# Layer norms of a two-block float32 network: order of the mean matmuls on TensorE and of the mean subtraction on VectorE

## What is computed

```python
def layer_norm(x, g, b):
    mu = jnp.mean(xf, axis=-1, keepdims=True)
    xc = xf - mu
    var = jnp.mean(xc * xc, axis=-1, keepdims=True)
    y = xc * lax.rsqrt(var + LN_EPS) * g + b
```

## Time and profile before

| | |
|---|---|
| Time, median of 3 executions | 1786.06 us (1785.59 to 1788.69) |
| Time of the profiled execution | 1788.76 us |
| Its span | 1787.0 us |
| Mean granted TensorE clock | 0.989 |
| TensorE matmul busy | 1742.0 us (97%) |
| VectorE busy | 1210.3 us (68%) |
| ScalarE busy | 978.1 us (55%) |
| GpSimd busy | 114.7 us (6%) |

### The profile page before, as it was taken

The page is one execution under the profiler, slowest core; times in us unless marked ns, Lnnn a source line. Parts: engine busy times, 40 slices in busy tenths (PEclk is TensorE's granted clock), DMA queues, the critical chain, the costliest instruction groups (busy, mean ns, idle before and its releaser), DMA issues.

```text
span 1787.0 us, 33465 instructions
## 1 busy us (share of the span) xinstructions
PE 1742.0 (97%) x11768; PEld 1579.9 (88%) x11768; DVE 1210.3 (68%) x2117; ACT 978.1 (55%) x1708; POOL 114.7 (6%) x124
## 2 busy tenths in 40 slices
PE   8999998999999999999899998999999999999998
PEld 7888998888899888888788888889999998888887
DVE  6776788777554776677777756776656467777764
ACT  5564595655355554466565635564434364565543
POOL 0001003000100000100300010003000100030001
PEclk9999999999999999999999999999999999999999
DMA  6665365456545666443446652433556534346662
GB/s 222 187 205 194 118 202 167 145 188 207 188 133 175 189 187 206 147 124 125 160 161 188 209 184 72 136 116 109 166 175 202 171 101 129 116 127 196 188 204 88
DMA packets 76640, 290.79 MB, mean 163 GB/s; under 512 B 9345, under 2 KB 11649, under 8 KB 76545
## 3 DMA queue, kind: packets, MB, share of 16 engines
q1 hardware_dynamic: 76544, 289.50, 51.1%
HBM read 288.42 MB, written 1.05 MB: 162 GB/s over the span
## 4 chain that ended last, share of the span: by engine, by line
PE 87%; DVE 5%; ACT 2%; issue 2%; POOL 2%; DMA 0%; SPq 0%; POOLq 0%; ACTq 0%; DVEq 0%
PE psum L518 33%; PE psum L519 17%; PE psum L510 10%; PE psum L512 10%; PE psum L511 10%; POOL sums L1059 2%; PE psum L650 1%; PE psum L759 1%; DVE r L1708 1%; PE psum L645 1%; DVE wlo L1554 1%; PE psum L882 1%; PE psum L889 1%; DVE r L1739 1%; ACT whi L1093 0%
## 5 line engine op out<-in xcount | busy, mean ns | idle before, releaser
L1554 DVE TENSOR_TENSOR wlo<-raw,whi 128x1024 fp32r<-128x1024 f32 (+3 forms) x496 | 648.0, 1314 | 292.4 <-ACT whi L1093 291.2
L518 PE MATMUL psum<-x_split,whi 128*128 128x512 f32 x1760 | 618.5, 395 | 6.0 <-DVE x_split L1589 3.4
L1093 ACT ACTIVATE whi<-raw 128x1024 fp32r<-128x1024 f32 (+3 forms) x496 | 548.7, 1119 | 40.0 <-PE psum L512 21.1
L519 PE MATMUL psum<-x_split,wlo 128*128 128x256 f32 x1760 | 494.3, 281 | 0.0
L518 PEld LDWEIGHTS psum<-x_split,whi 128*128 128x128 f32 x1760 | 331.0, 188 | 84.8 <-issue 3.6
L510 PE MATMUL psum<-x_split,whi 128*128 128x272 f32 (+1 forms) x1184 | 346.6, 293 | 4.4 <-DVE x_split L1744 4.4
L512 PE MATMUL psum<-x_split,wlo 128*128 128x272 f32 (+1 forms) x1184 | 338.5, 286 | 0.0
L511 PE MATMUL psum<-x_split,whi 128*128 128x272 f32 (+1 forms) x1184 | 337.6, 285 | 0.0
L519 PEld LDWEIGHTS psum<-x_split,wlo 128*128 128x128 f32 x1760 | 331.5, 188 | 0.0
L518 PE MATMUL psum<-h_split,whi 128*128 128x512 f32 x770 | 272.2, 397 | 0.0
L510 PEld LDWEIGHTS psum<-x_split,whi 128*128 128x128 f32 x1184 | 223.3, 189 | 14.7 <-issue 8.2
(11 more groups left out here) (231 smaller groups left out, 1748.0 us busy)
## 6 DMA issues: line engine op xcount, KB each, us to landing
raw<-w_in SPq DMA_DIRECT2D x264, 512.0 KB, 3.5
raw<-w_out SPq DMA_DIRECT2D x96, 704.0 KB, 4.3
raw<-w_mix SPq DMA_DIRECT2D x44, 512.0 KB, 3.6
raw<-w_rg SPq DMA_DIRECT2D x25, 512.0 KB, 4.1
raw<-w_q SPq DMA_DIRECT2D x24, 512.0 KB, 3.6
raw<-w_mixo SPq DMA_DIRECT2D x16, 576.0 KB, 3.7
raw<-w_kv SPq DMA_DIRECT2D x16, 512.0 KB, 3.6
raw<-w_rg_out SPq DMA_DIRECT2D x8, 640.0 KB, 4.1
```

Source lines behind the costliest of these rows:

```text
L518: nc.tensor.matmul(ps[:, bank, :], whi[slot][:, w], split, start=start, stop=False)
L519: return nc.tensor.matmul(part(bank, 0), wlo[slot][:, w], split[:, 0], start=False, stop=stop)
L1093: nc.scalar.activation(whi[slot][:, 0:cols], raw[slot][:, 0:cols], ACT.Copy).then_inc(w_hi_done, count)
L1554: V.tensor_tensor(wlo[slot][:, 0:cols], raw[slot][:, 0:cols], f(whi[slot][:, 0:cols]), ALU.subtract).then_inc(w_lo_done, 1)
```

## The change

On TensorE the token means now come first and in one run; the two means of all partitions come behind them, in the place of the six keep_warm matmuls (emb keeps its own order). On VectorE the centrings are in five parts instead of four: tile 0, tile 1, tiles 2 and 3, 4 and 5, 6 and 7. No centring stands ahead of the variance any more; centre(0) comes behind the reciprocal, and each of the others directly behind the scaling of the last tile of the part before it. Each scaling waits for its own part's centring. The counts that others wait for change from 4 to 5 a norm, and GpSimd and TensorE wait once more for work of the norm before.

```diff
+CENTRE_PARTS = ((0, 1), (1, 2), (2, 4), (4, 6), (6, 8))
+CENTRES = len(CENTRE_PARTS)
+CENTRE_OF = [c for c, (first, end) in enumerate(CENTRE_PARTS) for _ in range(first, end)]
...
             if name == "emb":
-                pe.wait_ge(xc_done, 4 * n)
+                pe.wait_ge(xc_done, CENTRES * n)
...
             else:
                 pe.wait_ge(sums_done, norm_stages.index(name) + 1)
-                means(sums[:, 0, :], first=True)
                 token_means(sums[:, 0, :], 0)
                 token_means(sums[:, 1, :], 4)
 
                 pe.wait_ge(acc_free, by_name[name].u0 + by_name[name].units)
-                means(r[:, KD - 1, :], last=True).then_inc(mean_done, 1)
                 token_means(r[:, KD - 1, :], 0)
                 pe.wait_ge(sq_done, KD * (n + 1))
                 ins = token_means(sq[:, KD - 1, :], 4, True)
             ins.then_inc(stat_done, 1)
-            keep_warm(6)
+            if name == "emb":
+                keep_warm(6)
+            else:
+
+                if n:
+                    pe.wait_ge(xc_done, CENTRES * n)
+                means(sums[:, 0, :], first=True)
+                means(r[:, KD - 1, :], last=True).then_inc(mean_done, 1)
             pe.wait_ge(rstd_done, n + 1)
...
                 pool.wait_ge(stat_done, n)
+                pool.wait_ge(mean_done, n)
...
-                    act.wait_ge(xc_done, 4 * n + k // 2 + 1)
+                    act.wait_ge(xc_done, CENTRES * n + CENTRE_OF[k] + 1)
...
-            def centre(k):
-
-                mean = acc(4, T).unsqueeze(1).broadcast_to([P, 2, T])
-                V.tensor_tensor(r[:, k:k + 2, t], r[:, k:k + 2, t], mean, ALU.subtract).then_inc(xc_done, 1)
-
-            dve.wait_ge(mean_done, n + 1)
+            def centre(c):
+
+                k, end = CENTRE_PARTS[c]
+                mean = acc(4, T).unsqueeze(1).broadcast_to([P, end - k, T])
+                V.tensor_tensor(r[:, k:end, t], r[:, k:end, t], mean, ALU.subtract).then_inc(xc_done, 1)
+
             if name == "emb":
-                for k in range(0, KD, 2):
-                    centre(k)
+                dve.wait_ge(mean_done, n + 1)
+                for c in range(CENTRES):
+                    centre(c)
...
             else:
-                centre(0)
-
                 ns = norm_stages.index(name)
...
             V.reciprocal(rstd_t[:, 0:nt], std_t[:, 0:nt]).then_inc(rstd_done, 1)
             if name != "emb":
-                centre(2)
-                centre(4)
+                dve.wait_ge(mean_done, n + 1)
+                centre(0)
             dve.wait_ge(spread, n + 1)
-            dve.wait_ge(xc_done, 4 * n + 3)
             v = version.get(name, 0)
             for k in range(KD + 1):
-                if k == 2 and name != "emb":
-                    centre(6)
-                if k == 6:
-                    dve.wait_ge(xc_done, 4 * n + 4)
                 if k < KD:
+                    dve.wait_ge(xc_done, CENTRES * n + CENTRE_OF[k] + 1)
                     V.scalar_tensor_tensor(r[:, k, t], r[:, k, t], par[:, C_G + KD * n + k:C_G + KD * n + k + 1],
                                            acc(6, T), ALU.mult, ALU.mult).then_inc(xn_done, 1)
+                    if name != "emb" and k < KD - 1 and CENTRE_OF[k + 1] != CENTRE_OF[k]:
+                        centre(CENTRE_OF[k + 1])
```

## The result

The changed kernel takes 1795.5 us (1791.1 to 1797.0) against 1786.5 for the kernel before: a ratio of 1.0049, 95% interval 1.0039 to 1.0059. That is 9.0 us more, where 4.6 more were forecast; the range ended at 1795.0.

The account below looks back on a forecast made before the run. TensorE holds 87% of the chain, but the end of VectorE's queue sets a norm's end. Terms 0.3 + 0.6 + 2.2 + 0.45 = 3.6, with the clock 4.6, added to the median 1786.06: 1790.7 us; range 1787.0 to 1795.0.

Parts of the forecast that it names:

- Statistics earlier: TensorE in a norm: with the mean pairs moved behind the tokens, the last token ends 0.78 us earlier.
- From the last token to the first scaling: In a 256-column norm: this stretch shortens by 0.49 us, with the first scaling waiting for the spread.
- VectorE's queue: Behind the first scaling of a 256-column norm: the queue to the last x_lo grows by 1.38 us.
- The late start of emb's means: At out3 and emb: the means wait for out3's last centring and start 2.16 us later.
- The clock at emb: TensorE's longer gap before emb's means makes them run partly at half clock: +1.0 us.
- The other norms: Later ends: +0.3 us for out0, out1 and out2, +0.6 for mixo0 and out4, +0.45 for out5.
- The one with more half-clock time: Rival: means fall into half clock in each of eight norms, losing 0.75 us each; 1796 us; 12%.
- The faster rival: At half clock TensorE binds, so earlier first tiles gain 0.48 us in eight norms; 1784.9 or 1782.7 us; 5%.
- The sum: Whole kernel: costs of 3.6 us, or 4.6 with the clock, added to the median of 1786.06 us.

Follow-up runs that it names:

- e1: Changed kernel with TensorE's half alone: VectorE centres by pairs, three pairs between reciprocal and first scaling; 1782.9 us, ratio 0.9980 to the kernel before.
- e5: Changed kernel with tiles 0 and 1 centred together again, four parts, otherwise interleaved as changed; 1790.9 us, ratio 1.0027 to the kernel before.
- e9: Kernel before with only the centring of tiles 6 and 7 moved from behind the first x_lo to ahead of it; 1784.9 us, ratio 0.9992.
- e4: Changed kernel with 26 more unused matmuls in TensorE's gap ahead of emb's means; 1791.5 us, ratio 1.0029 to the kernel before.
- e3: Changed kernel with emb's means in PSUM bank 3 instead of 4; 1789.0 us, ratio 1.0014 to the kernel before.
- e10: e3 plus unused matmuls while TensorE waits for GpSimd's sums in rg_out, o, mixo0 and mixo1; 1789.3 us, ratio 1.0018 to the kernel before.
- e11: e1 with emb's means in bank 3, plus the unused matmuls of e10 in the GpSimd waits; 1781.6 us, ratio 0.9971 to the kernel before.

## Why the prediction was wrong

- **Statistics earlier** (0.78 forecast). Measured 0.86: last token from 2.82 to 1.96 behind the last product; it is 0.86 too in rg_out, o and mixo1, where 0.89 stood. Only one of the two quick starts behind a mean pair was lost: four tokens on r take 0.45 instead of 0.36, but the first eight, now behind a product, take 0.81 as before.
- **From the last token to the first scaling** (0.49). Measured 0.50. The spread ends last now, the root came in time, and centre(0) is hidden: right.
- **VectorE's queue** (+1.38). Measured +1.36, with the forecast parts: scaling 1 starts 0.85 behind scaling 0, and the stall ahead of the first x_lo is gone. Right; the queue does set the end of a norm, as e1, e5 and e9 show from three sides. The six 256-column norms were priced at 0.3 together (out0, out1 and out2 at 0.11 each); these three and rg_out were 0.0.
- **The late start of emb's means** (2.16). Measured 2.12 in the trace (8.69 behind the last product instead of 6.57). Between e4 and e3 it is 1.69 at the end of the means and 2.5 by the medians. Right.
- **The clock at emb** (+1.0). This is the step that failed: right in kind and place, too small. The term took a quarter of the means at half clock as its value; in the trace they lose 1.67 (5.62 instead of 3.95). It left out that the half clock behind emb's own gap then lasts longer: it ended at 1107.6 in the earlier trace rows, ahead of the next products, and now at 1112.0, in them. By the traces of this place the term is about 2.1, by the medians of e4 and the kernel after 3.5 to 4.0.
- **The other norms** (0.3, 0.6 and 0.45, together 1.35). e3, where the gap is absent, is 3.0 over before (1.1 to 4.1), of which 0.41 is its means' later end. By the traces out5 is 0.25, just under the bounds of its term: its last scaling ends 0.67 later, as forecast, and most of that does not reach the end. mixo0 and out4 are 1.1 together where 0.6 stood. o and mixo1 were put at nothing and cost 1.0, the second miss: with half clock among the means and the spread the first scaling of o is not the full 1.4 earlier (5.98 behind the last product instead of 6.79), while the queue behind it is as much longer as elsewhere. In mixo1 the half clock of the kernel after covers 1589.9 to 1593.3, where before had full clock. e10 was to take the clock out of these norms and did not for rg_out, o and mixo1. Nor does one trace price such a norm: the last x_lo of mixo0 ends 17.19 behind the last product in the kernel after and 17.37 in e3, but 15.45 in e4, with the same code in this norm. So how much of this is the change and how much the chance of one trace stays open.
- **Rivals.** The one with more half-clock time had the sign and the size (1796) and half the place: it put the loss into the means of eight norms. In out0, rg_out, out1 and out2 the spread was not late; in o, mixo0, out4 and mixo1 the half clock of the kernel after does begin ahead of the means or in them, but all that these four lost is 2.1, against the rival's 0.75 in each of eight, and the largest loss is ahead of and in emb's means. The faster rival had nothing for it: earlier first tiles gained nothing in out0, out1 and out2.
- **The sum.** 4.6 with the clock at 3.5 to 4.0 instead of 1.0 is 7.1 to 7.6, with o and mixo1 8.1 to 8.6, against 9.0 (7.0 to 10.5). By the traces' smaller clock term about 2 us of the 9.0 have no place that I can show; part is the spread of single executions. The range ended too low, at 1795.0, for the same reason: its upper end had no room for a clock term of this size and half clock in other norms at once.

The rule on the cost of splitting ("VectorE: DVE Perf Modes" in the Trainium skill, errata section) held: 0.41 + 0.42 against 0.68. The statement of the same page of the Trainium skill (the section on the drain) that a semaphore between two Vector instructions costs nothing extra did not hold here: scaling 1 starts 0.04 behind the end of its centring, while unlinked instructions overlap by 0.08.

## What to carry to other kernels

When an engine's queue sets the end of a stage, work that it did while it waited is free, and moving it behind the wait costs all of it, however much earlier the first result then comes. Before spreading work through a queue, look for who waits on its last piece: here one bank, reused by the next norm, turned 2 us of reordering into a gap. And price a new gap on TensorE at the clock that the work behind it may get, with the next gap counted too; filling it with unused matmuls is a cheap trial. Here the best kernels took TensorE's new order and left three of the four pairs of centrings ahead of the first scaling: e11 is 4.3 us under the kernel before.

## What the runs showed of the hardware that was not expected

The size of the clock's part: with a gap of 3.6 instead of 0.6 us TensorE spent 12.8 us more at half clock per execution (50.3 against 37.5; the traces place 6.8 of it at emb), and filling the gap with unused matmuls gave 3.5 to 4.0 us back. Over 62 executions of the kernel before, time rises by 0.35 us with each microsecond of half clock, between 1783.5 and 1788.8 us; by this slope the 9.1 us less at half clock in e4 would be an estimated 3.2 us; in the kernel after the execution with the highest mean clock (0.990) took 1791.1 and the one with the lowest (0.984) 1797.0. The Trainium skill ("TensorE: Matmul & The Clock Gate", "Why this matters for your kernels") advises against gaps between bursts; e4 is that advice measured.

Filling a gap is not enough everywhere. In e10 TensorE worked with unused matmuls of 256 columns while it waited for GpSimd, and it was busy nearly all the time from the last product of o, and of rg_out, until the clock fell to half (window, its us, then busy us and count of PE, PEld, DVE, ACT, POOL; granted clock; DMA):

```profile
890.50:894.40 3.90, 3.83 (x32) 3.62 (x31) 1.43 (x2) 0.53 (x2) 1.70 (x2) 1.00 1.01 406
311.40:314.10 2.70, 2.67 (x24) 2.47 (x23) 0.48 (x2) 0.42 (x1) 0.65 (x1) 1.00 0.81 215
```

In e10 mixo0 kept full clock; in e11, with the same filling, rg_out kept it and mixo0 did not. What decides between them was not tested.
